# Fused mask-and-row-maximum pass in the softmaxes of two mixers, with the differential heads scaled at eviction

## The chip, the cores and the metric

One NeuronCore of a Trainium2 chip runs the whole program. The metric is the device time of one execution in microseconds, from three timed runs of the kernel before. Everything is float32 in memory; lower is better.

## The reference, cut to what matters

Two transformer blocks of two layers each are applied to 256 tokens of width 1024. The second block has an even and an odd layer, and their mixers hold the softmaxes that the change touches:

```python
def forgetting_attention(q, k, v, cum_logf):            # even layer, 8 heads of 64
    s = einsum(q_block, k[:qe]) * scale
    s = s + cum_logf[:, :, qs:qe, None] - cum_logf[:, :, None, :qe]
    p = softmax(where(causal, s, -inf)); out = p @ v

def differential_attention(q, k, v, lam):               # even layer, 4 heads, 2 scores each
    s = einsum(...) * scale                              # (h, j, q, k), j = 0, 1
    p = softmax(where(allowed, s, -inf))                 # allowed: by chunks of 64
    p = p[:, :, 0] - lam * p[:, :, 1]; out = p @ v       # then an RMS norm over the 128 columns of a head

def chunk_band_attention(q, k, v, rel_table):           # odd layer, 8 heads of 64
    s = einsum(...) * scale + bias                       # bias by relative distance, chunks masked
    p = softmax(s); out = p @ v
```

With 256 tokens there are two query blocks of 128: the first sees 128 keys, the second 256. So a head's scores are 128 rows by 384 columns, in one PSUM bank.

## The kernel before, in words

**The projections set the frame.** All weights are streamed once. A weight unit is 128 rows by up to 1024 columns: SyncE loads it to one of four `RAW` slots, ScalarE copies it to `WH` in the rounded matmul format (L1217, called a conversion below), VectorE computes the remainder `WL` = `RAW` - `WH` (L1479), and TensorE runs three 512-column matmuls for each 128x128 block of activations (L955, L956, L957: high times high, high times low, low times high). `WH` and `WL` have five slots, so ScalarE's conversion of unit u waits for `w_used`, that is until TensorE has finished unit u-5. Four PSUM banks `M` take the projections, four banks `AUX` everything else.

**The order is written by a planner.** `Plan` gives every step a due time in its own units (one unit is two sets of three matmuls). TensorE's and GpSimd's lists are sorted by that time, ScalarE's and VectorE's by the time plus an offset by kind (`LATER`). Each engine then runs its list strictly in order; semaphores join the lists. So a step that waits holds back all that stands behind it on its engine.

**The even mixer** (`even_mixer`, from about 985 to 1110 us) projects bq, af (8 forget gates), bk, bv, aq, ak, av. A projected head group is evicted and normalized (kind `hq`: four ScalarE instructions of 128x512, L1252 and L1256; `hn` on VectorE, L1622), turned by four TensorE transposes (kind `tq`, L1013) and evicted as queries or keys (L1277, to `QB`, `KB`, `QA`, `KA`).

- The forget gates become cumulative sums by row (`CT`) and by column (`NCT`, kind `cu2`, L1394 and L1395). GpSimd writes `NCT` to DRAM and reads it back broadcast over all partitions into `NB`, 128 x 8 heads x 384, by two DMAs (kind `nctld`, L1970 to L1974). Kind `nctma` on VectorE then adds the causal mask to two thirds of `NB`, in two passes of 128x1024 (L1871).
- The differential heads (`df_`), four of them, two scores (j = 0, 1) each. `df_s`: TensorE computes both scores (L1115 to L1118, the first of them waits for all of `QB` and `KB`); VectorE adds the chunk mask in PSUM (L1731), then takes the two negated row maxima (L1744, L1745); ScalarE takes the exponential with that bias and sums the rows (L1403, L1404). `df_p`: VectorE takes reciprocals (L1754), scales the first score's probabilities (L1761, L1762) and adds the second's, scaled (L1765, L1766). `pt`: TensorE transposes the result (L1125), ScalarE evicts it (L1419). `df_o`: TensorE multiplies by the values (L1136 to L1138), ScalarE evicts and squares (L1428 to L1434).
- The forgetting heads (`hg_`), four pairs, in the same steps: VectorE adds `CT` and `NB` by two instructions (L1738, L1740), takes the maxima (L1744, L1745); `hg_p` scales by the reciprocals (L1772 to L1777); `pt`, then `hg_o` (L1151, L1153).

**The odd mixer** (from about 1584 to 1637 us) has the `hg_` steps with a table `H` in place of `CT` and `NB`: one addition of 128x384 in PSUM (L1733), then the maxima.

Of the kernel before, what the change touches and what calls it, by code (L numbers as in the profile page):

```python
# [26 lines left out]
GAP = 3.9  # L27
LOG_EXP = "natural_log_exp_and_others"
# [193 lines left out]
class Plan:  # L222
# [456 lines left out]
    def even_mixer(self, S, lab, lab_o):  # L679
# [18 lines left out]
        ma = self.add("nctma", c.end + 24.0)  # L698
# [47 lines left out]
        self.CT, self.ct = S["CT"], ct  # L746
# [120 lines left out]
class Kernel:  # L867
# [4 lines left out]
    def __init__(self, nc, ctx, p):  # L872
# [29 lines left out]
        self.d_nct, self.d_nb = sem("d_nct"), sem("d_nb")  # L902
# [287 lines left out]
def scalar(e, k):  # L1190
# [9 lines left out]
    for s in p.for_act:  # L1200
# [191 lines left out]
        elif s.kind == "cu2":  # L1392
            e.wait_ge(k.aux_full[b], s.use)
            e.activation(s.NCT[0:8, :], aux[0:8, 0:256], ACT.Copy, scale=-1.0)  # L1394
            e.activation(s.CT[:, :], aux[:, 256:272], ACT.Copy).then_inc(k.aux_out[b], 1)  # L1395
        elif s.kind in ("df_s", "hg_s"):
# [6 lines left out]
            e.activation(x[:, 0:128], aux[:, 0:128], ACT.Exp, bias=s.m[:, 0:1], accum_out=s.sm[:, 0:1])  # L1403
            e.activation(x[:, 128:384], aux[:, 128:384], ACT.Exp, bias=s.m[:, 1:2], accum_out=s.sm[:, 1:2]).then_inc(k.aux_out[b], 1)  # L1404
# [19 lines left out]
        elif s.kind == "df_o":  # L1424
            e.wait_ge(k.aux_full[b], s.use)
            for t in range(T):
                x = aux[:, t * P:(t + 1) * P]
                e.activation(s.dst[t], x, ACT.Copy)  # L1428
                e.wait_ge(junk[0], junk[1])
                if t == 0:  # L1430
                    e.activation(p.JK[:, 0:P], x, ACT.Square, accum_out=s.bs[t]).then_inc(k.act_chain, 1)
                    chain += 1
                    junk = k.act_chain, chain
            e.activation(p.JK[:, 0:P], x, ACT.Square, accum_out=s.bs[t]).then_inc(k.aux_out[b], 1)  # L1434
# [19 lines left out]
def vector(e, k):  # L1454
# [5 lines left out]
    for s in p.for_dve:  # L1460
# [264 lines left out]
        elif s.kind in ("df_s", "hg_s"):  # L1725
            e.wait_ge(k.aux_full[b], s.use)
            if s.kind == "df_s":
                if s.n == 1:
                    e.wait_ge(k.d_c2, 16)
                v = aux[:, 0:512].rearrange("p (j c) -> p j c", j=2)[:, :, 0:P]  # L1730
                e.tensor_tensor(v, v, p.CHUNK.unsqueeze(1).to_broadcast([P, 2, P]), ALU.add).then_inc(k.dve_chain, 1)  # L1731
            elif s.extra is p.H:
                e.tensor_tensor(aux[:, 0:384], aux[:, 0:384], s.extra[:, s.h, :], ALU.add).then_inc(k.dve_chain, 1)  # L1733
            else:
                if s.n == 1:
                    e.wait_ge(k.aux_out[p.ct.bank], p.ct.use)
                ct = [p.CT[:, 8 * t + s.h:8 * t + s.h + 1] for t in range(T)]
                e.scalar_tensor_tensor(out=aux[:, 0:128], in0=aux[:, 0:128], scalar=ct[0], in1=s.extra[:, s.h, 0:P],  # L1738
                                       op0=ALU.add, op1=ALU.add)
                e.scalar_tensor_tensor(out=aux[:, 128:384], in0=aux[:, 128:384], scalar=ct[1], in1=s.extra[:, s.h, P:3 * P],  # L1740
                                       op0=ALU.add, op1=ALU.add).then_inc(k.dve_chain, 1)
            chain += 1
            e.wait_ge(k.dve_chain, chain)
            e.tensor_reduce(s.m[:, 0:1], aux[:, 0:128], AX.X, ALU.max, negate=True)  # L1744
            e.tensor_reduce(s.m[:, 1:2], aux[:, 128:384], AX.X, ALU.max, negate=True).then_inc(k.row_max, 1)  # L1745
# [3 lines left out]
        elif s.kind == "df_p":  # L1749
# [9 lines left out]
            rc = s.ss[0].rc  # L1759
# [441 lines left out]
```

## Time and profile before

| what | value |
|---|---|
| timed runs | 1910.91, 1912.83, 1914.89 us |
| median | 1912.83 us |
| profiled execution, span from first to last instruction | 1908.4 us |
| that execution's own time | not listed beside its span; the median of the runs stands 4.4 us above the span |
| TensorE matmul / weight load busy | 1880.6 / 1622.1 us |
| VectorE / ScalarE / GpSimd busy | 1300.4 / 1119.2 / 330.9 us |
| mean granted TensorE clock | 0.999 of full speed |
| HBM traffic | 224 GB/s over the span |

Busy time of TensorE is made of rows with modelled ends: a 512-column matmul is shown with 0.38 us while the next one starts 0.215 us later. An idle time shown on TensorE's rows is therefore some 0.16 us shorter than the real break in its stream. In a timeline row the columns are start, duration, engine, line, operation, output and inputs, and in brackets the idle time of the engine before the row with what ended it.

### The profile page before, as it was taken

The numbers are of one execution on the slowest core, as the hardware profiler recorded it, in microseconds if no ns is written. First come the engines' busy times: TensorE is split into PE (matmuls) and PEld (weight loads), VectorE is DVE, ScalarE is ACT, GpSimd is POOL, SyncE is SP. The second block draws the span as 40 slices with busy tenths as digits, with TensorE's granted clock in tenths as the row PEclk, the third lists the DMA queues.
The fourth block names the chain that finished last, engine by engine and source line by source line (L and its number), as shares of the span: only waits on it lengthen the run. The fifth ranks groups of instructions, "written<-read, shape, count | busy, mean of one in ns | idle before, by whom it ended". The sixth has DMA issues, their size and how long they took to land.

```text
span 1908.4 us, 24906 instructions
## 1 busy us (share of the span) xinstructions
PE 1880.6 (99%) x9073; PEld 1622.1 (85%) x9073; DVE 1300.4 (68%) x1919; ACT 1119.2 (59%) x1685; POOL 330.9 (17%) x559
## 2 busy tenths in 40 slices
PE   9999999999999999999999899999999999999999
PEld 7888888888888888888887688888888887788888
DVE  6687776666776776666568775776666578856664
ACT  6486555555866654655466665654555466665552
POOL 1110123111101441022100000431122111101220
PEclk9999999999999999999999999999999999999999
DMA  8866689868657997688865454997788787646884
GB/s 281 245 198 189 202 256 293 266 222 251 194 183 217 288 287 230 189 254 254 237 185 183 133 188 139 285 278 232 229 257 253 213 268 239 202 149 193 253 256 140
DMA packets 283497, 429.97 MB, mean 225 GB/s; under 512 B 25028, under 2 KB 161440, under 8 KB 283120
## 3 DMA queue, kind: packets, MB, share of 16 engines
q1 hardware_dynamic: 256144, 352.41, 59.8%
q0 software_dynamic: 26768, 75.64, 14.6%
q8 instruction: 72, 1.18, 0.3%
q14 instruction: 49, 0.40, 0.1%
q10 hardware_dynamic: 464, 0.34, 0.1%
HBM read 393.15 MB, written 35.15 MB: 224 GB/s over the span
## 4 chain that ended last, share of the span: by engine, by line
PE 86%; DVE 6%; ACT 4%; DMA 2%; issue 1%; POOL 0%; ACTq 0%; DVEq 0%
PE M L955 27%; PE M L957 27%; PE M L956 27%; DVE WL L1479 2%; ACT WH L1217 1%; PE AUX L999 1%; PE AUX L1186 1%; DMA TG<-squares 1%; PE AUX L1164 1%; DMA squares<-TG 1%; DVE SM L1665 1%; ACT TMP L1252 0%; DVE TMP L1622 0%; DMA RAW<-in_w_in 0%; PE AUX L1013 0%
## 5 line engine op out<-in xcount | busy, mean ns | idle before, releaser
L1479 DVE TENSOR_TENSOR WL<-RAW,WH 128x1024 fp32r<-128x1024 f32 (+1 forms) x670 | 810.5, 1215 | 447.9 <-ACT WH L1217 445.8
L1217 ACT ACTIVATE WH<-RAW 128x1024 fp32r<-128x1024 f32 (+1 forms) x670 | 704.1, 1054 | 528.7 <-PE M L957 480.5
L955 PE MATMUL M<-WH,Bh 128*128 128x512 f32 x1792 | 689.2, 385 | 2.0 <-DVE Bl L1506 1.7
L956 PE MATMUL M<-WL,Bh 128*128 128x512 f32 x1792 | 679.9, 379 | 0.0
L957 PE MATMUL M<-WH,Bl 128*128 128x512 f32 x1792 | 679.9, 379 | 0.0
L955 PEld LDWEIGHTS M<-WH,Bh 128*128 128x128 f32 x1792 | 339.2, 189 | 52.2 <-issue 3.2
L957 PEld LDWEIGHTS M<-WH,Bl 128*128 128x128 f32 x1792 | 339.1, 189 | 48.1
L956 PEld LDWEIGHTS M<-WL,Bh 128*128 128x128 f32 x1792 | 339.2, 189 | 45.8
L1247 ACT ACTIVATE AS<-M,KEEP 128x256 f32<-128x256 f32 x132 | 55.3, 470 | 78.3 <-PE M L957 78.2
L955 PE MATMUL M<-WH,MTh 128*128 128x512 f32 x128 | 52.9, 413 | 0.0
L1894 POOL TENSOR_TENSOR KEEP<-SM,KEEP 128x2 f32<-128x2 f32 x15 | 10.6, 710 | 219.9 <-DVE SM L1533 219.9
L956 PE MATMUL M<-WL,MTh 128*128 128x512 f32 x128 | 48.5, 379 | 0.0
L957 PE MATMUL M<-WH,MTl 128*128 128x512 f32 x128 | 48.5, 379 | 0.0
L1914 POOL DMA_DIRECT2D HB0t<-squares x48 | 26.3, 555 | 50.7 <-DMA squares<-HB0b 42.2
L1914 POOL DMA_DIRECT2D HD0t<-squares x48 | 26.4, 556 | 42.8 <-DMA squares<-HD0b 38.9
L1336 ACT ACTIVATE JK<-X 128x512 f32<-128x512 f32 x52 | 32.9, 633 | 1.3 <-DVE X L1543 0.5
L1914 POOL DMA_DIRECT2D HC1t<-squares x48 | 26.3, 554 | 41.4 <-DMA squares<-HC1b 41.4
L955 PE MATMUL M<-WH,FA0h 128*128 128x512 f32 x88 | 33.4, 379 | 0.0
L956 PE MATMUL M<-WL,FA0h 128*128 128x512 f32 x88 | 33.4, 379 | 0.0
L957 PE MATMUL M<-WH,FA0l 128*128 128x512 f32 x88 | 33.4, 379 | 0.0
L955 PE MATMUL M<-WH,FA1h 128*128 128x512 f32 x88 | 33.4, 379 | 0.0
L956 PE MATMUL M<-WL,FA1h 128*128 128x512 f32 x88 | 33.4, 379 | 0.0
(473 smaller groups left out, 2741.4 us busy)
## 6 DMA issues: line engine op xcount, KB each, us to landing
RAW<-in_ffn_w_in SPq DMA_DIRECT2D x352, 256.0 KB, 3.8
RAW<-in_w_in SPq DMA_DIRECT2D x103, 512.0 KB, 4.7
RAW<-in_w_gate_up SPq DMA_DIRECT2D x176, 256.0 KB, 4.4
RAW<-in_ffn_w_out SPq DMA_DIRECT2D x88, 512.0 KB, 4.6
RAW<-in_w_down SPq DMA_DIRECT2D x44, 512.0 KB, 4.7
RAW<-in_x_w_kv SPq DMA_DIRECT2D x32, 512.0 KB, 4.6
RAW<-in_even_w_in SPq DMA_DIRECT2D x24, 512.0 KB, 4.5
RAW<-in_odd_w_in SPq DMA_DIRECT2D x24, 512.0 KB, 5.2
```

Of the source, the lines that this page charges most:

```text
L955: e.matmul(out, s.hi, wh, start=s.at0, stop=False)
L956: e.matmul(out, s.hi, wl, start=False, stop=False)
L957: i = e.matmul(out, s.lo, wh, start=False, stop=s.final)
L999: tr = e.transpose(aux[:, i * P:(i + 1) * P], x, ident)
L1164: i = e.matmul(aux[:, t * 256:(t + 1) * 256], s.q[j][:, t * P:(t + 1) * P], s.k[j], start=j == 0, stop=j == 1)
L1186: i = e.matmul(aux[:, j * 256:(j + 1) * 256], s.v[j][kt], x[:, kt * 256:(kt + 1) * 256], start=kt == 0, stop=kt == 1)
L1217: e.activation(p.WH[:, h, 0:s.size], p.RAW[:, i, 0:s.size], ACT.Copy).then_inc(k.w_hi, 1)
L1247: e.activation(s.silu[t], banks[t][:, 0, :], ACT.Silu, scale=r[t]).then_inc(k.silu_made, 1)
L1336: e.activation(p.JK, s.srcs[t], ACT.Square, accum_out=s.ss[:, 2 * t + s.half:2 * t + s.half + 1]).then_inc(k.sq_sum, 1)
L1479: e.tensor_tensor(p.WL[:, h, 0:s.size], p.RAW[:, s.u % NRAW, 0:s.size], hi.bitcast(F32), ALU.subtract).then_inc(k.w_lo, 1)
L1665: e.tensor_reduce(s.ss[:, t * n:(t + 1) * n], sq.rearrange("p (g d) -> p g d", g=n), AX.X, ALU.add).then_inc(k.hq_sum, 1)
L1914: e.dma_start(x.rows[32 * c:32 * c + 32, :].rearrange("p (q e) -> p q e", q=q), p.parked[x.slot, c * n:(c + 1) * n].rearrange("(q j e) -> ...
```

## The change

- **Scores.** In `df_s` and `hg_s` the addition and the reduction become one VectorE instruction per block row, `tensor_tensor_reduce`: it writes -(scores + mask) and keeps the minimum of it by row, which is the negated maximum. There are two for each softmax (128 and 256 columns), each compiled to two instructions. The exponential gets `scale=-1`.
- **Forget gates.** The fused instruction takes one second operand, so `CT` must be in `NB` beforehand. A new ScalarE kind `nctq`, one step per head with two instructions (128x128 and 128x256), adds it in place. The first waits for both DMAs into `NB`. `nctma` now waits for all eight, and is due 1.5 units later.
- **Differential heads.** `df_p` no longer scales the first score's probabilities: the second's get the factor -lambda times both sums' quotient, and `df_o` scales by the first reciprocal as it evicts and squares.
- The constants are laid out so that mask operands of 128 and 256 columns exist.

```diff
-        ma = self.add("nctma", c.end + 24.0)
+        for h in range(8):
+            own = self.add("nctq", c.end + 17.0 + h)
+            own.NB, own.CT, own.h = S["NB"], S["CT"], h
+        ma = self.add("nctma", c.end + 25.5)
...
+        elif s.kind == "nctq":
+            if s.n == 1:
+                e.wait_ge(k.d_nb, 32)
+            h = s.h
+            e.activation(s.NB[:, h, 0:P], s.NB[:, h, 0:P], ACT.Identity, bias=s.CT[:, h:h + 1])
+            e.activation(s.NB[:, h, P:3 * P], s.NB[:, h, P:3 * P], ACT.Identity, bias=s.CT[:, 8 + h:9 + h]).then_inc(k.nb_own, 1)
...
-            e.activation(x[:, 0:128], aux[:, 0:128], ACT.Exp, bias=s.m[:, 0:1], accum_out=s.sm[:, 0:1])
+            e.activation(x[:, 0:128], aux[:, 0:128], ACT.Exp, bias=s.m[:, 0:1], scale=-1.0, accum_out=s.sm[:, 0:1])
...
-                e.activation(s.dst[t], x, ACT.Copy)
+                x, rc = aux[:, t * P:(t + 1) * P], s.pt.maker.ss[0].rc[:, t:t + 1]
+                e.activation(s.dst[t], x, ACT.Copy, scale=rc)
...
-                e.tensor_tensor(v, v, p.CHUNK.unsqueeze(1).to_broadcast([P, 2, P]), ALU.add).then_inc(k.dve_chain, 1)
-            elif s.extra is p.H:
-                e.tensor_tensor(aux[:, 0:384], aux[:, 0:384], s.extra[:, s.h, :], ALU.add).then_inc(k.dve_chain, 1)
...
-            e.tensor_reduce(s.m[:, 0:1], aux[:, 0:128], AX.X, ALU.max, negate=True)
-            e.tensor_reduce(s.m[:, 1:2], aux[:, 128:384], AX.X, ALU.max, negate=True).then_inc(k.row_max, 1)
+            e.tensor_tensor_reduce(aux[:, 0:128], aux[:, 0:128], own, -1.0, FAR, ALU.add, ALU.min, s.m[:, 0:1])
+            e.tensor_tensor_reduce(aux[:, 128:384], aux[:, 128:384], both, -1.0, FAR, ALU.add, ALU.min,
+                                   s.m[:, 1:2]).then_inc(k.row_max, 1)
...
-            e.tensor_scalar(s.nl, s.ss[1].rc, p.NLAM, None, ALU.mult)
-            e.tensor_scalar(x0[:, 0:128], x0[:, 0:128], rc[:, 0:1], None, ALU.mult)
-            e.tensor_scalar(x0[:, 128:384], x0[:, 128:384], rc[:, 1:2], None, ALU.mult).then_inc(k.dve_chain, 1)
+            e.scalar_tensor_tensor(out=s.nl, in0=s.ss[1].rc, scalar=p.NLAM, in1=s.ss[0].sm, op0=ALU.mult,
+                                   op1=ALU.mult).then_inc(k.dve_chain, 1)
...
-            e.wait_ge(*((k.d_nb, 32) if s.kind == "nctma" else (k.d_h, 48)))
+            e.wait_ge(*((k.nb_own, 8) if s.kind == "nctma" else (k.d_h, 48)))
```

TensorE's, GpSimd's and SyncE's lists are unchanged. The first place where the lists differ is ScalarE's, around the two evictions of turned bk to `KB`. A row is the line, the operation and its operands, with the semaphores that it waits for (their buffer counts behind). Before:

```order
L1217 ACTIVATE WH<-RAW 128x1024 [waits w_used_6,raw0_0]
L1277 ACTIVATE KB<-AUX 128x4x128 [waits aux_full3_14]
L1217 ACTIVATE WH<-RAW 128x1024 [waits w_used_6,raw1_1]
L1277 ACTIVATE KB<-AUX 128x4x128 [waits aux_full0_11]
L1217 ACTIVATE WH<-RAW 128x1024 [waits w_used_6,raw2_2]
L1403 ACTIVATE TMP,SM<-AUX,SM 128x128 [waits row_max_48]
L1404 ACTIVATE TMP,SM<-AUX,SM 128x256
```

With the change (`d_nb` is the semaphore of the two DMAs into `NB`; line numbers are of the changed file):

```order
L1280 ACTIVATE KB<-AUX 128x4x128 [waits aux_full3_14]
L1403 ACTIVATE NB<-NB,CT 128x128 [waits d_nb_86]
L1404 ACTIVATE NB<-NB,CT 128x256
L1403 ACTIVATE NB<-NB,CT 128x128
L1404 ACTIVATE NB<-NB,CT 128x256
L1220 ACTIVATE WH<-RAW 128x1024 [waits w_used_6,raw1_1]
L1280 ACTIVATE KB<-AUX 128x4x128 [waits aux_full0_11]
L1403 ACTIVATE NB<-NB,CT 128x128
L1404 ACTIVATE NB<-NB,CT 128x256
L1403 ACTIVATE NB<-NB,CT 128x128
L1404 ACTIVATE NB<-NB,CT 128x256
L1220 ACTIVATE WH<-RAW 128x1024 [waits w_used_6,raw2_2]
```

Two of the eight new steps, the first with the wait, now stand between the first and the second eviction of `KB`; two more stand behind the second; the other four follow one by one up to the end of the next `hq`.

The second place is VectorE's list in the first two differential heads. Before, the mask passes over `NB` stood ahead of the first head's `df_p`:

```order
L1479 TENSOR_TENSOR WL<-RAW,WH 128x1024 [waits w_hi_4]
L1871 TENSOR_TENSOR NB<-NB,C 128x8x128 [waits d_c2_105,d_nb_86]
L1871 TENSOR_TENSOR NB<-NB,C 128x8x128
L1754 RECIPROCAL SM<-SM 128x2 [waits aux_out2_17,su_lam_63,dve_chain_21]
L1754 RECIPROCAL SM<-SM 128x2 [waits aux_out1_16]
L1760 TENSOR_SCALAR SM<-SM,KEEP 128x2 [waits dve_chain_21]
```

With the change they stand between the two softmaxes of the second head (`nb_own` is counted up by the new ScalarE steps; a fused pass shows as two `ISA` rows):

```order
L1742 ISA AUX,SM<-AUX,C 128x128 [waits aux_full3_14]
L1742 ISA SM 128x1
L1743 ISA AUX,SM<-AUX,C 128x256
L1743 ISA SM 128x1
L1868 TENSOR_TENSOR NB<-NB,C 128x8x128 [waits d_c2_106,nb_own_87]
L1868 TENSOR_TENSOR NB<-NB,C 128x8x128
L1742 ISA AUX,SM<-AUX,C 128x128 [waits aux_full0_11,dve_chain_21]
L1742 ISA SM 128x1
```

The passes have moved behind the first head's `df_p` and ahead of the second head's.

## Rows read from the trace of the kernel before

**Rows 1.** The page, part 1: busy time by engine.

```profile
PE 1880.6 (99%) x9073; PEld 1622.1 (85%) x9073; DVE 1300.4 (68%) x1919; ACT 1119.2 (59%) x1685; POOL 330.9 (17%) x559
```

**Rows 2.** Windows: busy us of PE, PEld, DVE, ACT, POOL; clock, DMA share, GB/s.

```profile
1010.00:1060.00 50.00, 46.93 (x256) 37.63 (x255) 41.50 (x93) 36.06 (x97) 0.00 (x0) 1.00 0.51 168
...
1560.00:1640.00 80.00, 76.38 (x391) 62.42 (x390) 64.44 (x117) 52.11 (x97) 8.97 (x16) 1.00 0.73 224
```

**Rows 3.** Waits of TensorE, 1010 to 1060 us: total, times, longest.

```profile
PE AUX L1125 <- DVE TMP L1766: 2.5, 4, 1.2
```

**Rows 4.** DMA issues into `NB` with us to landing, and GpSimd's timeline.

```profile
NB<-forget_rows POOLq DMA_DIRECT2D x1, 1024.0 KB, 7.9
...
1004.80 0.89 POOL L1974 DMA_DIRECT2D NB<-forget_rows  x1 [0.58 <-issue]
```

**Rows 5.** Timeline of ScalarE, 1009 to 1022 us.

```profile
1009.23 0.60 ACT L1277 ACTIVATE KB<-AUX 128x512 f32<-128x512 f32 x1
1010.22 1.06 ACT L1217 ACTIVATE WH<-RAW 128x1024 fp32r<-128x1024 f32 x1 [0.39 <-PE M L957]
1011.24 0.60 ACT L1277 ACTIVATE KB<-AUX 128x512 f32<-128x512 f32 x1
1014.30 1.06 ACT L1217 ACTIVATE WH<-RAW 128x1024 fp32r<-128x1024 f32 x1 [2.46 <-PE M L957]
1015.27 0.35 ACT L1403 ACTIVATE TMP<-AUX,SM 128x128 f32<-128x128 f32 x1
...
1015.61 0.47 ACT L1404 ACTIVATE TMP<-AUX,SM 128x256 f32<-128x256 f32 x1
...
1016.89 1.06 ACT L1217 ACTIVATE WH<-RAW 128x1024 fp32r<-128x1024 f32 x1 [0.73 <-PE M L957]
...
1019.42 0.69 ACT L1252 ACTIVATE TMP<-M,KEEP 128x512 f32<-128x512 f32 x1 [0.67 <-PE M L957]
...
1021.93 1.04 ACT L1217 ACTIVATE WH<-RAW 128x1024 fp32r<-128x1024 f32 x1
```

**Rows 6.** Timeline of TensorE: first scores, then the transposes of heads 1 and 2.

```profile
1012.43 0.37 PE L1115 MATMUL AUX<-KB,QB 64*128 64x128 f32 x1
...
1023.29 0.55 PE L1125 MATMUL AUX<-CC,TMP 128*128 128x128 f32 x3 [0.26 <-DVE TMP L1766]
...
1033.60 0.55 PE L1125 MATMUL AUX<-CC,TMP 128*128 128x128 f32 x3 [0.48 <-DVE TMP L1766]
```

**Rows 7.** Timeline of VectorE, 1019 to 1034 us.

```profile
1019.12 2.35 DVE L1871 TENSOR_TENSOR NB<-NB,C 128x1024 f32<-128x1024 f32 x2
...
1023.15 1.22 DVE L1479 TENSOR_TENSOR WL<-RAW,WH 128x1024 fp32r<-128x1024 f32 x1
...
1025.68 0.42 DVE L1731 TENSOR_TENSOR AUX<-AUX,C 128x256 f32<-128x256 f32 x1
...
1026.68 0.42 DVE L1731 TENSOR_TENSOR AUX<-AUX,C 128x256 f32<-128x256 f32 x1
...
1031.83 0.22 DVE L1754 RECIPROCAL SM<-SM 128x2 f32<-128x2 f32 x2
...
1032.80 0.35 DVE L1765 SCALAR_TENSOR_TENSOR TMP<-TMP,SM 128x128 f32<-128x128 f32 x1
...
1033.47 0.42 DVE L1731 TENSOR_TENSOR AUX<-AUX,C 128x256 f32<-128x256 f32 x1
```

**Rows 8.** The odd mixer: additions to the scores by line, and a timeline row of TensorE.

```profile
L1733 DVE TENSOR_TENSOR AUX<-AUX,H x8: 531/556/567, 1587.0 to 1620.9; 128x384 f32<-128x384 f32 x8
...
1628.80 0.55 PE L1125 MATMUL AUX<-CC,TMP 128*128 128x128 f32 x3 [1.04 <-DVE TMP L1777]
```

**Rows 9.** TensorE's two longest breaks, and a window behind the first.

```profile
71.34 0.67 PE L1032 MATMUL AUX<-QT,KT 128*128 128x256 f32 x2 [2.13 <-ACT KT L1307]
...
70.00:80.00 10.00, 8.66 (x34) 7.38 (x35) 4.36 (x8) 3.96 (x6) 2.19 (x4) 0.83 0.97 279
...
1633.82 0.65 PE L1151 MATMUL AUX<-TMP,VD 128*64 128x256 f32 x4 [2.52 <-ACT TMP L1419]
```

More of the change, by code:

```diff
@@ L27 @@
 GAP = 3.9
+FAR = 3.0e38
 LOG_EXP = "natural_log_exp_and_others"
@@ L1402, in scalar @@
             e.wait_ge(k.row_max, s.m_n)
-            e.activation(x[:, 0:128], aux[:, 0:128], ACT.Exp, bias=s.m[:, 0:1], accum_out=s.sm[:, 0:1])
-            e.activation(x[:, 128:384], aux[:, 128:384], ACT.Exp, bias=s.m[:, 1:2], accum_out=s.sm[:, 1:2]).then_inc(k.aux_out[b], 1)
+            e.activation(x[:, 0:128], aux[:, 0:128], ACT.Exp, bias=s.m[:, 0:1], scale=-1.0, accum_out=s.sm[:, 0:1])
+            e.activation(x[:, 128:384], aux[:, 128:384], ACT.Exp, bias=s.m[:, 1:2], scale=-1.0, accum_out=s.sm[:, 1:2]).then_inc(k.aux_out[b], 1)
         elif s.kind == "cx_s":
@@ L1426, in scalar @@
             for t in range(T):
[L1427 to L1428 removed]
+                x, rc = aux[:, t * P:(t + 1) * P], s.pt.maker.ss[0].rc[:, t:t + 1]
+                e.activation(s.dst[t], x, ACT.Copy, scale=rc)
                 e.wait_ge(junk[0], junk[1])
                 if t == 0:
[L1431 removed]
+                    e.activation(p.JK[:, 0:P], x, ACT.Square, scale=rc, accum_out=s.bs[t]).then_inc(k.act_chain, 1)
                     chain += 1
                     junk = k.act_chain, chain
[L1434 removed]
+            e.activation(p.JK[:, 0:P], x, ACT.Square, scale=rc, accum_out=s.bs[t]).then_inc(k.aux_out[b], 1)
             junk = k.aux_out[b], s.use
@@ L1729, in vector @@
                     e.wait_ge(k.d_c2, 16)
-                v = aux[:, 0:512].rearrange("p (j c) -> p j c", j=2)[:, :, 0:P]
-                e.tensor_tensor(v, v, p.CHUNK.unsqueeze(1).to_broadcast([P, 2, P]), ALU.add).then_inc(k.dve_chain, 1)
-            elif s.extra is p.H:
-                e.tensor_tensor(aux[:, 0:384], aux[:, 0:384], s.extra[:, s.h, :], ALU.add).then_inc(k.dve_chain, 1)
-            else:
[L1735 to L1743, printed above, removed]
-            e.tensor_reduce(s.m[:, 0:1], aux[:, 0:128], AX.X, ALU.max, negate=True)
-            e.tensor_reduce(s.m[:, 1:2], aux[:, 128:384], AX.X, ALU.max, negate=True).then_inc(k.row_max, 1)
+                own, both = p.CHUNK, p.OPEN_CHUNK
+            else:
+                own, both = s.extra[:, s.h, 0:P], s.extra[:, s.h, P:3 * P]
+            e.tensor_tensor_reduce(aux[:, 0:128], aux[:, 0:128], own, -1.0, FAR, ALU.add, ALU.min, s.m[:, 0:1])
+            e.tensor_tensor_reduce(aux[:, 128:384], aux[:, 128:384], both, -1.0, FAR, ALU.add, ALU.min,
+                                   s.m[:, 1:2]).then_inc(k.row_max, 1)
         elif s.kind == "cx_s":
@@ L1865, in vector @@
         elif s.kind in ("nctma", "hmask"):
-            x, mask = (s.NB, p.CAUSAL[:, P:2 * P]) if s.kind == "nctma" else (p.H, p.CHUNK)
-            e.wait_ge(*((k.d_nb, 32) if s.kind == "nctma" else (k.d_h, 48)))
+            x, mask = (s.NB, p.CAUSAL) if s.kind == "nctma" else (p.H, p.CHUNK)
+            e.wait_ge(*((k.nb_own, 8) if s.kind == "nctma" else (k.d_h, 48)))
             e.wait_ge(k.d_c2, 16)
```

8 lines of the change are left out of this document (3 added, 5 removed).

## The prediction

> **What bounds the kernel now.** I read the page first, for the engine that never rests; then the windows of the three stretches with touched softmaxes, for what TensorE loses there; then the list of its waits; last the timelines of ScalarE, TensorE and VectorE around the first differential heads, for who is late. TensorE is busy 99% of the span, VectorE 68%, ScalarE 59% [rows 1]. The change takes nothing off TensorE's list, so only the breaks in its stream can shrink or grow. They are small: 3.07 us of idle in 1010 to 1060 us, 3.62 us in the odd mixer's stretch [rows 2]. An idle time shown on TensorE is some 0.16 us short of the real break (0.38 us shown for a matmul, 0.215 us from start to start). The transposes of the four differential heads wait for VectorE's last product: 2.5 us in four waits [rows 3], with 4 x 0.16 some 3.1 us. That and one break of 1.04 + 0.16 = 1.2 us in the odd mixer [rows 8] is all that shorter VectorE work can win here; the other breaks of 1060 to 1110 us and of the odd mixer follow a ScalarE step that itself waited for TensorE, and no touched instruction stands between.
>
> **The change, part by part.**
>
> *The new wait on ScalarE.* The second DMA into `NB` is issued at 1004.80 and lands 7.9 us later, at 1012.70 [rows 4]. Before, nobody needed it until VectorE's mask passes at 1019.12 [rows 7]. Now ScalarE stands at it as soon as it has evicted the first half of `KB`, at 1009.23 + 0.60 = 1009.83 [rows 5]. Behind the wait are queued two steps of `nctq`, one conversion and the second eviction of `KB`; and TensorE's first scores at 1012.43 [rows 6] need that eviction. The trace has no in-place addition on ScalarE. The nearest rows are the two exponentials of the same shapes with a column as bias: 0.35 and 0.47 us [rows 5], less some 0.1 us by which neighbours overlap, so 0.25 + 0.36 = 0.61 us for a step. Below that lies an eviction without overlap loss and without a bias column, some 0.42 us for both; above, 0.82 us without overlap. I take 0.61. Then: 1012.70 + 2 x 0.61 = 1013.92; conversion 0.97 (1014.30 to 1015.27 [rows 5]), 1014.89; eviction 0.60, 1015.49; with 0.1 us to TensorE, 1015.6. TensorE stands for 1015.6 - 1012.43 = **3.2 us** in place of going through.
>
> By the Trainium skill, ScalarE: Activation LUTs, section What ACT_TABLE_LOAD costs, an ACTIVATE with a column as bias takes about 280 ns + 0.833 ns a column and neighbours overlap by 93 ns; by it, as an estimate, a step is 0.69 us and the break 3.3 us. No row here has this instruction, so the sum keeps 0.61.
>
> *ScalarE up to the next conversion.* From here ScalarE is the late one. The conversion of 1014.30 waited for TensorE, so it starts at 1014.30 + 3.2 = 1017.5. From there, in the new order: conversion 0.97, step 0.61, exponentials 0.8 (two instructions with their sums), step 0.61, conversion 0.97, step 0.61, exponentials 0.8: 1022.87, where TensorE's shift alone would have 1019.42 + 3.2 = 1022.62. Then `hq` 2.51 (1019.42 to 1021.93), step 0.61, conversion to its end 1.06: 1027.05. VectorE's remainder of that unit, at 1023.15 before [rows 7], starts at 1027.1, 3.95 us late. The first head's transposes lose their break (0.26 + 0.16 us), since the mask passes no longer stand in front of them.
>
> *VectorE's chain to the second head's transposes.* Before, VectorE is busy without a break from 1023.15 to TensorE's transposes at 1033.60: 10.45 us. Into this stretch the mask passes move: +2.35 us [rows 7]. Out of it come two old score treatments of 1.00 us each (1025.68 to 1026.68: addition and two maxima). The fused pass is not in the trace. Nearest are the two-operand products of 128 and 256 columns, 0.67 us for the pair (1032.80 to 1033.47 [rows 7]), plus two reads of the row result; a small VectorE instruction takes 0.08 to 0.1 us of the queue. So 0.84 us, 0.16 us saved each, 0.32 together. Bounds: 0.67 if the reads cost nothing; 1.5 us if the pass runs at half speed. In `df_p` 0.97 us lie between the first reciprocal and the first product (1031.83 to 1032.80); now 0.26 + 0.25 for reciprocals and factor, 0.46 us saved. New chain: 10.45 + 2.35 - 0.32 - 0.46 = 12.02, end at 1027.1 + 12.0 = 1039.1 against 1033.60: TensorE is now **5.5 us** behind.
>
> *What comes back.* In the third head one score treatment and `df_p` stand on the path (0.16 + 0.46), in the fourth two and `df_p` (0.32 + 0.46): 1.4 us of breaks that exist [rows 3]. The forgetting heads save 0.48 us a softmax (two additions 0.67, then maxima), but VectorE idles there before each conversion it waits for, and ScalarE waits for TensorE: counted as nothing; if all of that cover went, 1 us at most. In the odd mixer an addition of 0.556 us [rows 8] and maxima become 0.84, 0.29 us saved; two such stand in VectorE's unbroken stretch ahead of the break at 1628.80: 0.6 us. The differential heads' evictions get a column as scale, some 0.4 us a head on ScalarE, beside waits for row maxima: nothing.
>
> Sum without the clock: +5.5 - 1.4 - 0.6 = **+3.5 us**.
>
> *The clock.* At 71.34 TensorE came out of a break of 2.13 us shown, and the ten microseconds from 70 have a mean granted clock of 0.83 [rows 9]: part of them ran at 1.2 GHz in place of 2.4, and (1 - 0.83) x 10 = 1.7 us were lost. A break of 2.52 us shown at 1633.82 [rows 9] left the clock full: 1.00 over 1560 to 1640 [rows 2]. So such breaks can go either way; the new one, 3.2 - 0.16 = 3.0 us shown, is longer than both, and I hold a fall likelier than not. ScalarE's lateness of 0.25 us hides a little: +1.7 - 0.25 = +1.5 us.
>
> Sum: 3.5 + 1.5 = **+5.0 us**. The profiled span of 1908.4 becomes 1913.4. The median of the runs stands 4.4 us above the span; I carry that over: 1912.8 + 5.0 = **1917.8 us**. A measurement of this kernel can tell about 0.2%, or 3.8 us, from no change.
>
> **The rivals.**
>
> 1. *The same break without the clock's fall*: +3.5, 1916.3 us. For it: the row at 1633.82. Against it: the new break is longer.
> 2. *Faster: the wait costs nothing.* If both DMAs land before ScalarE comes, the second eviction of `KB` is late by 1.22 us of steps and hides in the 0.6 us of slack before 1012.43. Then TensorE loses 0.6 us there, the first head gives 0.4, the second stays (+2.35 of masks against an earlier start), third and fourth give 1.4, the odd mixer 0.6: -1.8, with the reads free about -3, so 1910 to 1911 us. It decides at 1009.83: the landing would have to come 2.9 us earlier. Against it: the DMA's issue, and all ahead of it, is unchanged, and it landed at 1012.70 [rows 4].
> 3. *The fused pass is slow*, 1.5 us in place of 0.84: +0.66 each on the chain, seven on the path (two, one and two in the differential heads, two in the odd mixer), +4.6: 1921 to 1922 us. For it: nothing in the trace shows this instruction. Against it: every two-operand row runs near one column per ns. The Trainium skill, Vector Engine (DVE) Microarchitecture Reference, section Points that are easy to get wrong, says that the scalar-tensor-tensor shape with two SBUF sources wider than bf16 halves its throughput. Here one source is in PSUM, so by the letter it does not apply; no row here has the forbidden case with an accumulator.
> 4. *The change doesn't do what it says*: the minimum and the later scaling could need other waits than listed. The lists show the same semaphores but the new one; I give it no chance of its own.
>
> **How the numbers follow.** Fall of the clock 42%, rival 1 33%, rival 2 12%, rival 3 13%. Range: at the bottom the step at 0.42 us (four in the break and behind it, -0.8), the forgetting heads' 1 us, and part of rival 2's distance: 1912.5. At the top, the sum with passes dearer by half of rival 3: 1920.5. Slower by over 0.2%: 36 of the 42, 15 of the 33, 11 of the 13, 62%. Faster by over 0.2%: 3% of rival 2 and 1% for the unknown, 4%. The rest, 34%, is within.
>
> **What would show it.** In the changed profile: an idle time of some 2.9 us on ScalarE before the first addition to `NB`, released by the DMA; a break of some 3 us on TensorE before its first scores of `KB` and `QB`, released by the eviction to `KB`; VectorE unbroken from about 15 us later to the second head's transposes, with the mask passes inside; a clock at the lower level behind the break, or not; fused rows of about 0.35 and 0.48 us with small reads. I am wrong if ScalarE passes the first addition without waiting, if TensorE's first scores need no wait, or if fused rows take over 0.6 and 0.8 us.

## The result, and the profile after

The changed kernel's median is 1915.23 us (1912.53 to 1916.94, 10 runs) against 1910.26 us (1907.69 to 1914.89, 10 runs) of the kernel before, measured with it: a ratio of 1.0023, 95% interval 1.0014 to 1.0033, so some 4.4 us slower, 2.7 to 6.3. The profiled execution took 1916.94 us and has a span of 1914.6 us.

Busy time by engine from the page of the changed kernel; VectorE has 12.6 us less than in [rows 1], ScalarE 6.9 us more, and neither says anything on the result:

```profile
PE 1886.7 (99%) x9073; PEld 1626.6 (85%) x9073; DVE 1287.8 (67%) x1927; ACT 1126.1 (59%) x1701; POOL 330.9 (17%) x559
```

Line numbers are now those of the changed file: 3 more than before on TensorE and on ScalarE up to about L1400, then 9 more, and from VectorE's score passes on 3 fewer (L1766 is L1763). The timeline of ScalarE, which answers to [rows 5] (start, duration, engine, line, operation, output and inputs, then the idle time and what ended it):

```profile
1007.67 0.60 ACT L1280 ACTIVATE KB<-AUX 128x512 f32<-128x512 f32 x1
1011.59 0.40 ACT L1403 ACTIVATE NB<-NB,CT 128x128 f32<-128x128 f32 x1 [3.32 <-DMA NB<-forget_rows]
1011.90 0.49 ACT L1404 ACTIVATE NB<-NB,CT 128x256 f32<-128x256 f32 x1
1012.30 0.39 ACT L1403 ACTIVATE NB<-NB,CT 128x128 f32<-128x128 f32 x1
...
1012.99 1.04 ACT L1220 ACTIVATE WH<-RAW 128x1024 fp32r<-128x1024 f32 x1
1013.93 0.57 ACT L1280 ACTIVATE KB<-AUX 128x512 f32<-128x512 f32 x1
...
1018.19 1.06 ACT L1220 ACTIVATE WH<-RAW 128x1024 fp32r<-128x1024 f32 x1 [2.30 <-PE M L960]
```

The wait is there, with the queue behind it in the order that was forecast: two steps of additions, a conversion, the second eviction to `KB`. The waits of TensorE over 1008 to 1060 us, which answer to [rows 3], and its timeline at the two places of [rows 6]:

```profile
PE AUX L1118 <- ACT KB L1280: 3.9, 1, 3.9
PE AUX L1128 <- DVE TMP L1763: 1.6, 1, 1.6
```

```profile
1014.87 0.55 PE L1118 MATMUL AUX<-KB,QB 64*128 64x128 f32 x1 [3.92 <-ACT KB L1280]
...
1040.24 0.55 PE L1128 MATMUL AUX<-CC,TMP 128*128 128x128 f32 x3 [1.61 <-DVE TMP L1763]
```

With 0.16 us each, the first is a real break of 4.1 us where there was none, the second 1.8 us where there were 0.6. Then the windows behind the first break (busy time of PE, PEld, DVE, ACT, POOL, then the granted clock):

```profile
1010.00:1015.00 5.00, 1.08 (x7) 0.65 (x5) 0.94 (x1) 3.41 (x8) 0.00 (x0) 0.84 0.84 307
1015.00:1020.00 5.00, 5.00 (x16) 3.65 (x17) 1.75 (x6) 2.70 (x7) 0.00 (x0) 0.50 0.39 109
1020.00:1025.00 5.00, 5.00 (x24) 4.11 (x23) 2.88 (x10) 4.51 (x14) 0.00 (x0) 0.97 0.40 105
```

TensorE came out of the break at the lower level, 1.2 GHz, and stayed there for all of 1015 to 1020 us: 2.5 us lost, and 0.15 in the next window. Busy time reads 5.00 of 5.00 there, as at full speed; only the count of matmuls (16, against 26 in 1015 to 1020 of the kernel before) and the clock's column show it. Last VectorE, which answers to [rows 7]:

```profile
1028.71 1.23 DVE L1488 TENSOR_TENSOR WL<-RAW,WH 128x1024 fp32r<-128x1024 f32 x1 [3.00 <-ACT WH L1220]
...
1031.24 0.29 DVE L1742 CUSTOM_DVE_ANT_0 AUX<-AUX,C 128x128 f32<-128x128 f32 x1
1031.45 0.14 DVE L1742 DVE_READ_ACCUMULATOR2_ANT SM<- 128x1 f32 x1
1031.45 0.46 DVE L1743 CUSTOM_DVE_ANT_0 AUX<-AUX,C 128x256 f32<-128x256 f32 x1
1031.83 0.14 DVE L1743 DVE_READ_ACCUMULATOR2_ANT SM<- 128x1 f32 x1
1031.83 2.35 DVE L1868 TENSOR_TENSOR NB<-NB,C 128x1024 f32<-128x1024 f32 x2
...
1040.10 0.29 DVE L1742 CUSTOM_DVE_ANT_0 AUX<-AUX,C 128x128 f32<-128x128 f32 x1
```

A score treatment takes 0.59 us of the queue (1031.24 to 1031.83): the read of the row result stands beside the next pass and costs nothing of its own. The mask passes sit in the middle of the second head's chain.

**Where the time went.** I measured each break of TensorE from start to start of neighbouring matmuls, beyond 0.215 us, in both traces. From the first scores of `KB` and `QB` on, the changed kernel's trace is 7.8 us longer: (1914.6 - 1010.8) - (1908.4 - 1012.4), the second number of each being the place where TensorE was ready for them. Over 1005 to 1112 us its breaks sum to 13.3 us against 9.4; in the odd mixer's stretch 3.1 against 4.1; the clock behind the first break took 2.6. That makes 3.9 - 1.0 + 2.6 = 5.5. The rest of the 7.8 is a wait of 0.9 us for VectorE at 1672.97 and a second fall of the clock at 1638 us, 1.7 us (8.1 in all, 0.3 too much). Both stand in traces of some of the kernels below and not of others, with the change and without it, so I count neither to the change: 5.5 us, and 4.4 (2.7 to 6.3) by the timed runs.

### The profile page after: what moved, and what is told of

Same layout as the page of the kernel before. It is cut to its first block, busy times and chain, and to the rows that moved or that the text cites. A ratio compares the mean times of both kernels' runs of the same rounds, so it can differ in the third digit from the quotient of the medians.

```text
span 1914.6 us, 24930 instructions
## 1 busy us (share of the span) xinstructions
PE 1886.7 (99%) x9073; PEld 1626.6 (85%) x9073; DVE 1287.8 (67%) x1927; ACT 1126.1 (59%) x1701; POOL 330.9 (17%) x559
## 4 chain that ended last, share of the span: by engine, by line
PE 85%; DVE 5%; ACT 4%; DMA 3%; issue 2%; POOL 0%; ACTq 0%; DVEq 0%; POOLq 0%
PE M L958 27%; PE M L960 26%; PE M L959 26%; DVE WL L1488 2%; ACT WH L1220 1%; PE AUX L1002 1%; PE AUX L1189 1%; PE AUX L1167 1%; DMA TG<-squares 1%; DMA squares<-TG 1%; ACT TMP L1255 1%; DVE SM L1674 1%; DMA NB<-forget_rows 0%; DMA SQI<-squares 0%; DMA RAW<-in_w_in 0%
```

## The experiments

The theory: the wait in ScalarE's queue breaks TensorE's stream, the clock falls behind the break, and the mask passes lengthen the chain of the second head; against that, the fused passes and the later scaling shorten the other chains. The main rival: the additions cost as work on ScalarE, or the fused passes cost, wherever they stand. The kernel before was timed again with each of the three groups of experiments: medians 1910.92, 1910.77 and 1911.29 us. This is what the ten kernels of the experiments gave, under the two that they are compared with; breaks are real ones, in us, of the profiled executions.

| kernel | median | ratio to before (95%) | first scores | first head's output | second head's transposes | odd mixer, transposes |
|---|---|---|---|---|---|---|
| before | | 1 | 0 | 0 | 0.6 | 1.2 |
| changed | 1915.23 | 1.0023 (1.0014 to 1.0033) | 4.1, clock falls | 0.6 | 1.8 | 0.2 |
| bare wait | 1913.09 | 1.0012 (1.0003 to 1.0020) | 2.6 | 0 | 0.6 | 1.2 |
| break filled | 1913.62 | 1.0011 (1.0002 to 1.0020) | 3.8, of it 3.0 filled | 1.0 | 1.8 | 0.2 |
| masks late only | 1914.04 | 1.0017 (1.0008 to 1.0026) | 3.8, clock falls | 0.6 | 0.6 | 0.2 |
| adds behind `KB` | 1911.24 | 1.0001 (0.9992 to 1.0010) | 0 | 2.4 | 1.8 | 0.2 |
| adds behind `KB`, masks late | 1908.40 | 0.9990 (0.9981 to 0.9998) | 0 | 1.0 | 0.6 | 0.2 |
| adds behind first head | 1910.97 | 0.9997 (0.9988 to 1.0006) | 0 | 0.2 | 1.0 | 0.2 |
| fused pass only | 1908.95 | 0.9986 (0.9977 to 0.9995) | 0 | 0 | 0.3 | 0.2 |
| no forgetting part | 1906.30 | 0.9978 (0.9969 to 0.9987) | 0 | 0.1 | 0.3 | 0.2 |
| adds on GpSimd | 1908.84 | 0.9988 (0.9977 to 0.9998) | 0 | 0.2 | 1.8 | 0.2 |
| the same, masks late | 1906.53 | 0.9970 (0.9956 to 0.9983) | 0 | 0.2 | 0.3 | 0.2 |

### The wait alone

```diff
+        self.add("nctw", c.end + 17.0)
         ma = self.add("nctma", c.end + 24.0)
...
+        elif s.kind == "nctw":
+            e.wait_ge(k.d_nb, 32)
```

> The kernel before, and on ScalarE at the place of the first addition only the wait for the second DMA into NB; no addition and nothing else of the change. Theory: ScalarE stands till the landing at 1012.7, then conversion 0.97 and eviction 0.60: TensorE's first scores at 1014.4 in place of 1012.4, and all behind it 1.9 us later; +1.9 us without a fall of the clock (1912.2), +3.5 with it (1913.8). Rival (the landing is hidden, the additions themselves make the break): +0.5 us or less, 1910.8.

ScalarE's timeline at the wait, TensorE's at the first scores, and the window behind them:

```profile
1012.87 1.06 ACT L1218 ACTIVATE WH<-RAW 128x1024 fp32r<-128x1024 f32 x1 [3.21 <-DMA NB<-forget_rows]
```

```profile
1014.77 0.34 PE L1116 MATMUL AUX<-KB,QB 64*128 64x128 f32 x1 [2.43 <-ACT KB L1278]
```

```profile
1015.00:1020.00 5.00, 5.00 (x28) 4.16 (x27) 3.43 (x8) 2.63 (x6) 0.00 (x0) 1.00 0.48 135
```

The break is there without any addition, 2.6 us of it, at full clock behind it (28 matmuls, 1.00), and the time is 2.3 us above before (0.6 to 3.8), 2.2 by the medians. The rival is out: the landing is not hidden. The break is longer than the 1.9 us expected for two reasons. The landing is no fixed distance from TensorE: it came 0.27 us after TensorE was ready in the kernel before (1012.70 against 1012.43), some 0.7 us after it here (1012.85 against 1012.17), and 0.75 us after it in the changed kernel (issued at 1003.13, 8.4 us to landing by the DMA view, 1011.53 against 1010.78). And TensorE's first scores start 0.36 us behind the end of the eviction to `KB` (1014.41 to 1014.77), where 0.1 had been taken; the changed kernel has the same 0.36 (1014.51 to 1014.87).

### The clock behind the break

Here TensorE also multiplies a warm-up tile that nobody reads.

```diff
+            if s.kind == "df_s" and s.n == 1:
+                if s.use > 1:
+                    e.wait_ge(k.aux_out[b], s.use - 1)
+                for _ in range(28):
+                    e.matmul(aux[:, 0:256], p.WARM[:, 0:P], p.WARM[:, 0:256], start=True, stop=True)
             for x in s.turned:
```

> The changed kernel, and TensorE multiplies the warm-up tile 28 times (256 columns, some 3 us at the full clock) while it stands before the first scores of KB and QB; nothing waits for less than before. Theory (the low clock behind the break costs on the path): granted clock 1.00 over 1015 to 1020 us in place of 0.50, ScalarE's next conversion comes 1.45 us sooner behind the scores, and the time is 1.5 to 2.6 us below the change: 1913.2 us (1912.5 to 1913.9). Rival (the slow columns hide under ScalarE's lateness): within 0.5 us of the change, 1915.

TensorE's timeline, ScalarE's next conversion, and the window behind:

```profile
1012.77 3.23 PE L1114 MATMUL AUX<-WARM 128*128 128x256 bf16 x28
1016.59 0.34 PE L1123 MATMUL AUX<-KB,QB 64*128 64x128 f32 x1 [0.59 <-ACT KB L1285]
```

```profile
1018.45 1.06 ACT L1225 ACTIVATE WH<-RAW 128x1024 fp32r<-128x1024 f32 x1 [0.85 <-PE M L960]
```

```profile
1015.00:1020.00 5.00, 4.41 (x30) 3.47 (x28) 2.42 (x6) 4.15 (x9) 0.00 (x0) 1.00 0.51 152
```

From the first scores to that conversion: 1018.45 - 1016.59 = 1.86 us, and 1018.19 - 1014.87 = 3.32 us in the changed kernel. That is the 1.45 us of the expectation. From the scores to the second head's transposes 23.2 us against 25.4, 2.2 us less. The median is 1.6 us below that of the changed kernel, the ratio 2.3 us less; the two intervals overlap (1.0014 to 1.0033, and 1.0002 to 1.0020), so the size rests on the trace and the timed runs agree with it. The rival that the slow columns hide under ScalarE is out: ScalarE itself waits for TensorE there, 2.30 us in the changed kernel.

### The mask passes alone

```diff
-        ma = self.add("nctma", c.end + 25.5)
+        ma = self.add("nctma", c.end + 32.2)
```

> The changed kernel with the two mask passes alone moved into the third head's stretch on VectorE; the additions and the wait stay in place. Theory (break and mask passes are separate costs): break of some 4 us and low clock stay, the second head's break of 1.77 us falls by the 1.2 us that the two versions without the break showed, and one of 0.25 stays: 1.2 to 1.5 us below the change, 1913.8 us. Rival (VectorE is late by so much behind the break that the passes decide nothing): 1915.

TensorE's timeline at the first scores and at the second head's transposes:

```profile
1017.28 0.34 PE L1118 MATMUL AUX<-KB,QB 64*128 64x128 f32 x1 [3.59 <-ACT KB L1280]
...
1040.18 0.55 PE L1128 MATMUL AUX<-CC,TMP 128*128 128x128 f32 x3 [0.40 <-DVE TMP L1763]
```

The break before the scores stays (3.8 us, low clock behind it); the one before the second head's transposes falls from 1.8 to 0.6 us, and the 0.25 us before the transposes of `hq` that stood ahead of it goes. 1.5 us by the breaks, 1.2 by medians and ratios, as expected. By the timed runs alone, whose intervals overlap, it would not be shown, and the clock differs too: in this profiled execution it was low for 3.4 us behind the break (1.7 us lost), in the changed kernel's for 5.4. The share of the masks rests on the breaks; the two versions with GpSimd below, which differ in the place of the masks alone, show it again.

### The additions behind the second eviction of KB

```diff
-            own = self.add("nctq", c.end + 17.0 + h)
+            own = self.add("nctq", c.end + 18.7 + 0.75 * h)
```

> The additions to NB start behind the second eviction of KB (8 steps, 0.75 us apart in the plan), the mask passes stay where the change has them. Theory (the wait for the DMA breaks TensorE, the clock falls behind that break): the break of 4.1 us before the first scores of KB and QB goes back to the 1.2 us or less of the kernel before, the granted clock stays at 0.95 or more over 1010 to 1020 us; the mask passes still stand in the second head's chain, so its transposes wait some 2 to 2.6 us. Sum against the kernel before: +1.9 there, -1.4 in heads three and four, -0.6 in the odd mixer: about 0, 1910.3 us (1909 to 1911.5), some 5 us below the change. Rival (the sixteen additions as work on ScalarE, or the fused passes, are what costs): no part of that moves, so 1914 us or more.

The time is that of the kernel before to 0.1 us, the break and the fall of the clock are gone, and the second head's transposes wait as in the changed kernel. But a break stands where none was expected, on TensorE behind this step of ScalarE (one timeline row of each):

```profile
1025.47 0.47 ACT L1428 ACTIVATE TMP<-AUX 128x384 f32<-128x384 f32 x1
```

```profile
1026.04 0.46 PE L1139 MATMUL AUX<-VB,TMP 128*128 128x128 f32 x2 [2.24 <-issue]
```

The profile puts the wait down to "issue"; but the row starts 0.1 us after ScalarE's eviction of the first head's transposed probabilities ends (1025.94). ScalarE was late for it: eight steps of additions between 1011.9 and 1021.1 us, 0.70 us each. The DMA is not what made it late: ScalarE still stands 0.88 us at it ahead of the first addition, but the conversion behind the first two steps starts 1.96 us after TensorE was ready for the scores, as in the kernel before. So the additions behind it do cost as work in that stretch. That half of the rival holds: the additions are hidden by nothing where ScalarE has no idle time. By the breaks it is 2.4 + 0.25 + 1.8 - 1.05 = +3.4 us up to the second head and -1.9 and -1.0 behind it, +0.5 in all, where I had expected +1.9 and -2.0: the sum was right, and both of its parts were too small.

The same with the additions further apart and the mask passes late:

```diff
-            own = self.add("nctq", c.end + 17.0 + h)
+            own = self.add("nctq", c.end + 19.0 + 1.5 * h)
...
-        ma = self.add("nctma", c.end + 25.5)
+        ma = self.add("nctma", c.end + 32.2)
```

> The additions start behind the second eviction of KB, 1.5 us apart in the plan, and the mask passes go into the third head's stretch, where VectorE waits for conversions. Theory: no break before the first scores, no fall of the clock, 2.35 us less in the second head's chain: -2 to -3 us against the kernel before, 1908 us (1907 to 1909). Rival (additions as work on ScalarE): 1913 us or more. Second rival (VectorE has no real idle time in the third head, the masks only move the lateness there): as the run with the masks left in place, 1910 us.

1908.40 us, 1.9 us below before (0.4 to 3.6): breaks of 1.0 and 0.6 us are left where 2.4 and 1.8 stood. VectorE does have the idle time in the third head. The first head's output comes ahead of the moved masks on VectorE, so its smaller break goes to the spacing of the additions; the spacing alone was not tried.

### Additions behind the first head

```diff
-            own = self.add("nctq", c.end + 17.0 + h)
+            own = self.add("nctq", c.end + 28.0 + 1.2 * h)
...
-        ma = self.add("nctma", c.end + 25.5)
+        ma = self.add("nctma", c.end + 38.5)
```

> The additions begin behind the first differential head's eviction (planned 28.0 us behind the gate's projection and 1.2 us apart), the mask passes go into the fourth head's stretch. Theory (an addition costs only where ScalarE is late, which is up to the first head's output): the breaks of the version without the forgetting part, 0.14 us before the first output of a head and 0.3 before the second head's transposes: -4 to -5 us against the kernel before, 1906.3 us (1905.3 to 1907.3). Rival (sixteen additions cost wherever they stand): as the version with the first additions behind KB, 1908 us or more.

This expectation failed. The stretch before the first head's output is clean, and TensorE's timeline has new breaks in the heads behind it (and one of 0.9 us before the fourth's transposes):

```profile
1031.55 0.55 PE L1128 MATMUL AUX<-CC,TMP 128*128 128x128 f32 x3 [0.79 <-DVE TMP L1763]
1034.21 0.49 PE L1139 MATMUL AUX<-VB,TMP 128*128 128x128 f32 x2 [0.38 <-ACT TMP L1428]
...
1044.90 0.49 PE L1139 MATMUL AUX<-VB,TMP 128*128 128x128 f32 x2 [1.59 <-ACT TMP L1428]
```

ScalarE is busy 59% of the span but 24.7 of the 30 us from 1030 in the version without the forgetting part, and 27.1 with the additions. I had taken the waits for row maxima in its timeline for cover; they stand at fixed places, and in this trace ScalarE runs without a break through two steps of additions, two conversions and the eviction that the third head's output waits for (1040.73 to 1044.85). "Which is up to the first head's output" was wrong: the additions that were put behind it delayed outputs up to the third head. The mask passes moved too, to the fourth head's stretch, so its 0.9 us need not be the additions'.

### Without the forgetting part, and the fused pass alone

The kernel before with the new passes for the differential heads and the odd mixer and the later scaling; the forgetting heads keep their two additions and maxima. In the second version the later scaling is undone too.

```diff
-        for h in range(8):
-            own = self.add("nctq", c.end + 17.0 + h)
-            own.NB, own.CT, own.h = S["NB"], S["CT"], h
-        ma = self.add("nctma", c.end + 25.5)
+        ma = self.add("nctma", c.end + 24.0)
...
+        elif s.kind == "hg_s" and s.extra is not p.H:
+            e.wait_ge(k.aux_full[b], s.use)
...
```

> The kernel before with the fused passes of the differential heads and of the odd mixer and the later scaling of the differential heads; the forgetting part is as before (no additions on ScalarE, its masks at the old place, its softmaxes in the old form). Theory: these parts only take time off VectorE's chains: 0.41 us a treatment and 0.46 us a head, against 3.1 us of breaks before transposes and 1.2 us in the odd mixer: -2 to -3 us, 1908 us (1907 to 1909). Rival (the fused pass or the scaling eviction costs on the path): 1910.5 us or more.

> The kernel before with the fused passes of the differential heads and the odd mixer alone; the differential scaling is as before, and so is the forgetting part. Theory (seven treatments on the path at 0.41 and more of saving each, capped by the breaks): the odd mixer's break of 1.20 us falls to 0.20, and the differential heads lose 1.2 to 1.8 us of 3.1: 2.2 to 2.8 us below the kernel before, 1908.3 us; the later scaling is worth the other 1.5 to 2. Rival (all of the gain is the later scaling): 1909.8 us or more.

Without the forgetting part: 1906.30 us, 4.2 us below the kernel before (2.5 to 5.9). The list of TensorE's waits over 1008 to 1060 us has one row left, on an eviction that the change does not touch:

```profile
PE AUX L1116 <- ACT QA L1278: 0.5, 1, 0.5
```

The breaks before the transposes of the four heads were 0.42, 0.63, 0.72 and 1.34 us and are 0, 0.28, 0.26 and 0.13; the odd mixer's 1.20 is 0.20. That is 3.4 us. With the fused pass alone they are 0.43, 0.29, 0.71, 0.58 and 0.20: 2.1 us, and the timed runs give 2.7 (1.0 to 4.4) by ratio and 1.8 by medians. So the later scaling is worth about 1.3 us by the breaks. In the first and the third head the fused pass alone gives nothing (0.43 and 0.71), the scaling all.

### The additions on GpSimd

```diff
-        elif s.kind == "nctq":
-            if s.n == 1:
-                e.wait_ge(k.d_nb, 32)
-            h = s.h
-            e.activation(s.NB[:, h, 0:P], s.NB[:, h, 0:P], ACT.Identity, bias=s.CT[:, h:h + 1])
-            e.activation(s.NB[:, h, P:3 * P], s.NB[:, h, P:3 * P], ACT.Identity, bias=s.CT[:, 8 + h:9 + h]).then_inc(k.nb_own, 1)
...
+        elif s.kind == "nctq":
+            if s.n == 1:
+                e.wait_ge(k.d_nb, 32)
+            h = s.h
+            e.tensor_scalar(s.NB[:, h, 0:P], s.NB[:, h, 0:P], s.CT[:, h:h + 1], None, ALU.add)
+            e.tensor_scalar(s.NB[:, h, P:3 * P], s.NB[:, h, P:3 * P], s.CT[:, 8 + h:9 + h], None, ALU.add).then_inc(k.nb_own, 1)
```

> The changed kernel with the sixteen additions to NB on GpSimd behind its own loads of NB; mask passes where the change has them. GpSimd has no work from the loads to 1114 us. Theory (the wait and the work hurt because they stand in ScalarE's queue): no break before the first scores, clock 1.00 there, no wait of 2.4 us for the first head's copies; only the mask passes stand in the second head's chain, 1.2 to 1.5 us: 1907.8 us (1907 to 1909), between the version without the forgetting part (1906.3) and the kernel before. Rival 1 (GpSimd needs over 1 us an addition, so that VectorE waits for the last of them before its mask passes): a new break before the second head's transposes, 1911 us or more. Rival 2 (GpSimd's passes slow VectorE's down): VectorE's passes of 1012 to 1030 us are longer by 10% or more.

> As the version with the additions on GpSimd, and the mask passes in the third head's stretch. Theory: nothing of the forgetting part is on the path any more: the breaks of the version without it, 1906.3 us (1905.3 to 1907.3), 4 to 5 us below the kernel before. Rival (the passes cost what they cost in the chain wherever they stand): as the version with the masks in the second head, 1907.8.

With the masks where the change has them 1908.84 us; with `nctma` at `c.end + 32.2` as above 1906.53 us, 5.7 us below before by ratio (3.2 to 8.4), 4.8 by medians. So the whole change, with the additions on GpSimd and the masks later, is faster than both kernels; it is level with the version without the forgetting part, and its breaks are the same to 0.1 us. GpSimd's timeline in it:

```profile
1010.94 0.61 POOL L1963 TENSOR_SCALAR NB<-NB,CT 128x128 f32<-128x128 f32 x1 [6.95 <-DMA NB<-forget_rows]
1011.54 0.92 POOL L1964 TENSOR_SCALAR NB<-NB,CT 128x256 f32<-128x256 f32 x1
...
1016.36 1.64 POOL L1963 TENSOR_SCALAR NB<-NB,CT 128x128 f32<-128x128 f32 x1
...
1024.54 0.92 POOL L1964 TENSOR_SCALAR NB<-NB,CT 128x256 f32<-128x256 f32 x1
```

GpSimd stands 6.95 us at the same DMA and nobody is behind it. In the version with the masks early the last addition ends at 1025.02 and VectorE did wait 0.85 us for it (rival 1 of that expectation, in small: a step takes 1.5 us where GpSimd is undisturbed, not over 2), and the second head's transposes waited 1.8 us as in the changed kernel, with 1.0 us before the transposes of `hq` ahead of them. Rival 2 (VectorE slowed down by 10%) is out but for single instructions; they are shown at the end.

## Why the prediction was right or wrong

Forecast +5.0 us and 1917.8 us; measured 1915.23 us, +4.4 by the ratio (2.7 to 6.3), +5.0 by the medians. The 2.6 us by which the absolute number is too high are the starting point's: the median of three runs that it was told from, 1912.83, is 2.6 us above that of ten. In every timed run of the kernel before whose own span is on record the time stands 1.8 to 1.9 us above the span. So the profiled span of 1908.4 us was that of a run of some 1910.3 us, and the 4.4 us that the forecast carried over were too many.

1. **The new wait, 3.2 us: mechanism right, size 4.1.** ScalarE stood 3.32 us, released by the DMA. Of the missing 0.9 us the largest part, 0.5 us, is the landing against TensorE's place (0.27, then 0.75 us), which the forecast held fixed. Another 0.26 is TensorE's start behind the eviction, 0.36 us in place of 0.1. The last 0.2 are the two steps of additions: 0.70 us each (1011.59 to 1012.30, 1012.99), not 0.61, which was taken from exponentials that read PSUM. The estimate from the Trainium skill (ScalarE: Activation LUTs, section What ACT_TABLE_LOAD costs) has 0.69 us for a step, and this trace agrees.
2. **ScalarE's chain to 1027.1: sized too short.** From the conversion behind the scores to VectorE's remainder 10.5 us (1018.19 to 1028.71) in place of 9.6: four steps dearer by 0.09, and a wait of 0.49 us for TensorE, which ran at the low clock. The forecast's "ScalarE's lateness of 0.25 us hides a little" had it the wrong way round: ScalarE followed TensorE, so the slow clock went through to it.
3. **VectorE's chain, 12.02 us: right.** 1028.71 to 1040.24 is 11.53; the difference is two treatments at 0.59 in place of 0.84. The mask passes are inside. The run with the masks alone moved confirms that they cost 1.2 to 1.5 us, less than their 2.35, since a late ScalarE is the next in line: with the masks gone VectorE stands 0.76 us for a conversion in that chain.
4. **What comes back, 1.4 and 0.6 us: 1.9 and 1.0.** The treatment was mis-sized: the read of the row result is hidden behind the next pass, so that 0.41 us and not 0.16 are saved in a differential head, and 0.54 in the odd mixer, where the break of 1.20 fell to 0.20. The forgetting heads gave nothing, as forecast: the breaks of 1.8, 0.9 and 1.9 us between 1061 and 1096 us are in every trace.
5. **The clock, +1.5: it fell, and cost 2.2 to 2.6.** The estimate came from a stretch in which the low clock lasted some 3.4 us; here it lasted some 5.4. In the run with the masks alone moved it lasted 3.4 us behind nearly the same break, so how long it lasts is not fixed by the change, and 1.7 us would have been as possible.

In sum, to the second head's transposes the changed kernel lost 8.2 us of TensorE's time (breaks 6.7 against 1.05, clock 2.6) where the forecast had 5.5 + 1.5 = 7.0, and won 2.9 where it had 2.0. The errors are 1.2 and 0.9 us and of opposite sign: +5.3 by the traces (5.5 above, where a small break at 1106 us is counted too), +5.0 forecast. Right in mechanism, in sign and in sum; the sum owes something to luck.

**The rivals.** The break without the clock's fall was realized by the bare wait, whose break is shorter. "The wait costs nothing" is out. The slow fused pass is out: 0.29 and 0.46 us, faster than the forecast; the two-source rule of the Trainium skill's Vector Engine (DVE) Microarchitecture Reference, section Points that are easy to get wrong, was argued not to apply with one source in PSUM, and no halving shows in these rows. The differential heads' evictions went from 0.277 to 0.368 us for 128 columns, 0.09 us for the scale column; the same section of ScalarE: Activation LUTs gives 93 ns for such an operand, and this trace agrees. Hidden, as forecast. The bottom of the range took four cheaper steps of additions where the forecast's own chain has six (-0.8 in place of -1.1); nothing hangs on it.

**What the forecast did not price**: the additions as work. They were taken to cost where they stand ahead of something late, and 16 of them looked small against ScalarE's 59%. Behind the second eviction of `KB`, where the wait no longer stops TensorE, they still made breaks of 2.4, 1.0, or 0.5 and 1.75 us, at the three places that were tried in ScalarE's list. In the changed kernel this was covered by the break itself (0.6 us at the first output), so the sum did not suffer. Taking the runs apart by breaks: fused passes -2.1, later scaling -1.3, masks +1.5, and wait and additions with the clock +7.4, which no run has alone (it is what the changed kernel's breaks and clock show up to the second head, less the masks and the 0.4 us of the version without the forgetting part): +5.5.

## What to carry to other kernels

Before a step is moved to another engine, look for the wait that it brings and ask what stands behind it in that engine's list; an engine that is idle in that stretch (GpSimd here: its timeline in the kernel before has nothing from 1006 to 1109 us) can stand 7 us at a DMA for nothing, where the same wait on a busy one stops the program. The mean busy share is no measure of cover: read the windows of the stretch, and find the place where each idle time stands. A break of TensorE costs its length and, where the clock falls, 1.7 to 2.7 us more in these traces; keeping the array busy through it gave that part back in the one run that tried it.

## What the runs showed of the hardware

**The same break may or may not let the clock fall.** In the odd mixer every one of these twelve kernels has the break of 2.7 us behind which [rows 9] show 2.52. Behind it the clock fell to the lower level in eight profiled executions and stayed full in four, the kernel before among them. One microsecond, one to two behind the break's end, in the changed kernel and then in the kernel before:

```profile
1639.00:1640.00 1.00, 1.00 (x4) 0.82 (x3) 0.35 (x1) 0.00 (x0) 0.00 (x0) 0.50 0.95 356
```

```profile
1635.00:1636.00 1.00, 1.00 (x6) 0.89 (x5) 0.42 (x1) 0.48 (x2) 0.00 (x0) 1.00 0.87 340
```

Each such fall lasted some 3.4 us and cost about 1.7. At 71 us breaks of 2.1 to 2.4 us were followed by a fall in all five executions that had them, those of 1.9 us and less in none of the seven others. So a break's length does not decide by itself, and part of the spread of 6 to 9 us between executions of the kernel before can be whether the clock fell at these places; a difference of 1.7 us between single profiled executions says nothing by itself.

**GpSimd and VectorE slow each other down, but not in the fused pass.** In the version with GpSimd's additions and late masks, and in the one with early masks, two-operand products of VectorE with both operands in SBUF took up to 0.55 us for 0.35 (128 columns) and 0.62 for 0.48 (256), and GpSimd's 128-column additions up to 1.64 us for 0.60; the fused passes, one operand of which is in PSUM, kept their 0.29 (once 0.33) and 0.47 us. GpSimd's long additions, at 1013.92, 1016.36 and 1021.85 us, stand beside VectorE's remainders `WL` = `RAW` - `WH`, whose two operands are in SBUF as well. VectorE's timeline in the version with late masks:

```profile
1015.14 0.47 DVE L1737 CUSTOM_DVE_ANT_0 AUX<-AUX,C 128x256 f32<-128x256 f32 x1
...
1018.04 0.55 DVE L1756 SCALAR_TENSOR_TENSOR TMP<-TMP,SM 128x128 f32<-128x128 f32 x1
```

The Trainium skill, GPSIMD Engine Reference, section 1. Specifications, says that the two share their SBUF interfaces, with contention for VectorE's instructions with two SBUF inputs; by that rule, the trace agrees. The cost here was up to 0.2 us on instructions of VectorE that no break of TensorE waited for.

**Left open.** Whether the second fall of the clock, at 1638 us, is made likelier by anything in the change was not tried; with eight of twelve it shows no pattern by kernel. Nor was a shorter way from the gates to the landing tried, which would leave the additions on ScalarE without a wait.
